# Two-layer decoder trunk with a routed expert mixer: order of x's reloads, of the scatters and of the gathers between the layers

## The reference, cut to what matters

```python
h = rms_norm(x, norm1_gain[l]);  z = h @ w_in[l]        # q, k, v, u: 512 columns each
att, pool = dilated_attention(q, k, v), pool_mixer(u, ...)
x = x + concat([att, pool]) @ w_out[l]
x = x + hier_moe(rms_norm(x, norm2_gain[l]), ...)        # each token goes to 2 of 16 experts
```

## Time and profile before

| | us |
|---|---|
| median of three runs | 1723.12 |
| the profiled execution | 1723.27 |
| its span, from the first instruction to the last | 1721.4 |
| PE busy | 1491.7 |
| DVE busy | 781.1 |
| ACT busy | 452.3 |
| POOL busy | 315.3 |

### The profile page before, as it was taken

The page is one execution under the profiler, slowest core; times in us unless marked ns, Lnnn a source line. Parts: engine busy times, 40 slices in busy tenths (PEclk is TensorE's granted clock), DMA queues, the critical chain, the costliest instruction groups (busy, mean ns, idle before and its releaser), DMA issues.

```text
span 1721.4 us, 22556 instructions
## 1 busy us (share of the span) xinstructions
PE 1491.7 (87%) x6963; PEld 1079.8 (63%) x6964; DVE 781.1 (45%) x1883; ACT 452.3 (26%) x886; POOL 315.3 (18%) x204
## 2 busy tenths in 40 slices
PE   5999978998992999999289998899999749999990
PEld 4878867886882444444178786788778624444440
DVE  5777656663336122212267866656533452212210
ACT  4231245662111011111222222567412101111110
POOL 1000068001000122222500001930200012222224
PEclk9999989999995999999599999899999869999995
DMA  8000020000168499973870002000002945999947
GB/s 314 19 1 0 0 98 1 2 1 1 73 222 291 156 283 298 341 223 89 226 222 0 1 0 98 1 1 2 1 25 90 330 154 160 270 301 280 311 91 162
DMA packets 116624, 221.09 MB, mean 128 GB/s; under 512 B 5976, under 2 KB 72736, under 8 KB 116544
## 3 DMA queue, kind: packets, MB, share of 16 engines
q1 hardware_dynamic: 91744, 131.82, 22.2%
q0 software_dynamic: 19136, 69.38, 16.4%
q10 hardware_dynamic: 5664, 18.88, 2.8%
HBM read 170.77 MB, written 49.28 MB: 128 GB/s over the span
## 4 chain that ended last, share of the span: by engine, by line
PE 77%; DVE 7%; issue 6%; DMA 3%; ACT 2%; POOL 1%; ACTq 1%; DVEq 0%; PEld 0%; PEldq 0%; POOLq 0%; SPq 0%
PE ps L1566 19%; PE ps L1360 17%; PE ps L1340 11%; PE ps L1493 9%; PE ps L1579 9%; PE ps L1446 7%; PE ps L1420 2%; DMA out_x<-x_res,arena 2%; PE ps L1507 2%; PE ps L1422 1%; POOL out_x L622 1%; DVE arena L1149 1%; PE ps L1480 1%; DVE w_in_lo L944 1%; DMA big<-in_w_in 1%
## 5 line engine op out<-in xcount | busy, mean ns | idle before, releaser
L1566 PE MATMUL ps<-big,arena 128*128 x720 | 325.8, 606 | 9.6 <-issue 8.3
L1340 PE MATMUL ps<-cst,arena 128*128 128x128 f32 x1242 | 186.4, 284 | 76.4 <-DVE arena L915 37.6
L905 DVE TENSOR_TENSOR arena<-ps,par 128x512 f32<-128x512 f32 x126 | 81.2, 686 | 355.8 <-PE ps L1340 355.8
L1566 PEld LDWEIGHTS ps<-big,arena 128*128 128x128 f32 x720 | 135.7, 194 | 170.4 <-issue 170.4
L1340 PEld LDWEIGHTS ps<-cst,arena 128*128 128x128 f32 x1242 | 152.6, 146 | 122.7 <-DVE arena L915 39.3
L1360 PE MATMUL ps<-w_in_hi,hT_hi 128*128 128x512 f32 x512 | 206.1, 402 | 12.7 <-DVE hT_lo L933 9.9
L1360 PE MATMUL ps<-w_in_hi,hT_lo 128*128 128x512 f32 x512 | 202.1, 395 | 0.0
L1360 PE MATMUL ps<-w_in_lo,hT_hi 128*128 128x512 f32 x512 | 201.9, 394 | 0.0
L614 POOL DMA_INDIRECT x_res<-token_rows,row_tok x62 | 61.0, 985 | 605.1 <-issue 309.2
L1579 PE MATMUL ps<-big,arena 128*128 x360 | 163.8, 598 | 5.4 <-issue 5.4
L1446 PE MATMUL ps<-big,arena 128*128 128x64 f32 x1152 | 149.7, 278 | 0.0
(11 more groups left out here) (169 smaller groups left out, 1770.1 us busy)
## 6 DMA issues: line engine op xcount, KB each, us to landing
big<-in_w_gate SPq DMA_DIRECT2D x32, 1024.0 KB, 10.6
big<-in_w_up SPq DMA_DIRECT2D x32, 1024.0 KB, 13.1
big<-in_w_down SPq DMA_DIRECT2D x32, 1024.0 KB, 15.3
big<-in_w_in SPq DMA_DIRECT2D x16, 1024.0 KB, 9.5
big<-in_w_out SPq DMA_DIRECT2D x4, 2048.0 KB, 10.3
token_rows<-arena ACTq DMA_DIRECT2D x16, 512.0 KB, 3.3
out_x<-x_res ACTq DMA_DIRECT2D x16, 512.0 KB, 4.1
x_res<-out_x SPq DMA_DIRECT2D x8, 512.0 KB, 5.8
```

What stands on the lines that cost most here:

```text
L905: ins = ve.tensor_tensor(out=dst[:, 4 * h:4 * h + 4, :], in0=ps[:, banks + h, :].rearrange("p (a c) -> p a c", c=P), in1=spread(gain[:, 4 ...
L1340: ins = te.transpose(ps[:, bank + i // 4, (i % 4) * P:(i % 4 + 1) * P], src, ident)
L1566: ins = te.matmul(ps[:, 2, :], xgT[:, k, :], big[:, ds(at + k * 2 * FE, 2 * FE)], start=k == 0, stop=k == K - 1)
```

## The change

SP's order between the layers is turned round: it now waits for the used blocks' scatters itself, loads x's tiles 0 and 1, steps the new semaphore `spare_may`, and only then loads the two parts of w_in. Tiles 2 to 4 wait for the gathers alone, tiles 5 to 7 for all scatters, and wpool comes last. ACT's Else branch waits for `spare_may` before it lets a spare scatter go. GpSimd waits itself, in every `add_rows` but block 0's, until all earlier scatters have landed, then steps `y_free` (which takes `y_whole`'s place for the evacuations of y) and waits for the two halves of y. The gathers get a bound on the row, and empty rows are given a row number above it, so that they are skipped. `y_whole` and `x_whole` are gone.

```diff
@@ -424,6 +424,7 @@
             sp.sem_inc(w_loaded, BIAS)
+            sp.sem_inc(spare_may, BIAS)
             sp.dma_start(xr[:, 0, :], x[0, 0:P, :]).then_inc(s_x[0], 16)
...
@@ -449,29 +450,34 @@
                     used = sp.value_load(start_i[0:1, NE:NE + 1], min_val=2 * SEQ // P, max_val=BLOCKS)
-                    sp.wait_ge(dn_done, upto(l, BLOCKS, used - BLOCKS))
-                    load_in(l, 1, 2)
-                sp.wait_ge(pm_done, upto(l, 2 * NG, 0))
-                sp.dma_start(wpool[:, :, :], w_pool[ds(l, 1), :, :, :].rearrange("a g c e -> c (a g) e"))\
-                    .then_inc(s_wpool, 16)
-                with sp.If(l > 0):
-                    sp.wait_ge(x_whole, upto(l, 1, 0))
+                    sp.wait_ge(s_add, upto_added(0, used))
                     sp.sem_inc(s_passed, 1)
                     for t in range(2):
                         sp.dma_start(xr[:, t, :], out[t * P:(t + 1) * P, :]).then_inc(s_again[t], 16)
+                    sp.sem_inc(spare_may, 1)
+                    sp.wait_ge(dn_done, upto(l, BLOCKS, used - BLOCKS))
+                    load_in(l, 1, 2)
                     for t in range(2):
                         sp.wait_ge(s_again[t], l * 16)
                         sp.sem_inc(x_ready, 1)
                     for i in range(RING):
                         sp.wait_ge(s_xg[i], l * (16 * USES[i]))
                         sp.sem_inc(s_passed, 1)
+                    for t in range(2, 2 + RING):
+                        sp.dma_start(xr[:, t, :], out[t * P:(t + 1) * P, :]).then_inc(s_again[t], 16)
+                    for t in range(2, 2 + RING):
+                        sp.wait_ge(s_again[t], l * 16)
+                        sp.sem_inc(x_ready, 1)
                     sp.wait_ge(s_add, upto_added(l, 0))
                     sp.sem_inc(s_passed, 1)
-                    for t in range(2, T):
+                    for t in range(2 + RING, T):
                         sp.dma_start(xr[:, t, :], out[t * P:(t + 1) * P, :]).then_inc(s_again[t], 16)
-                    for t in range(2, T):
+                    for t in range(2 + RING, T):
                         sp.wait_ge(s_again[t], l * 16)
                         sp.sem_inc(x_ready, 1)
+                sp.wait_ge(pm_done, upto(l, 2 * NG, 0))
+                sp.dma_start(wpool[:, :, :], w_pool[ds(l, 1), :, :, :].rearrange("a g c e -> c (a g) e"))\
+                    .then_inc(s_wpool, 16)
                 sp.wait_ge(rows_t, 1)
...
@@ -613,11 +620,17 @@
                         out=xg[slot], out_offset=None, in_=token_rows,
-                        in_offset=bass.IndirectOffsetOnAxis(ap=row_tok[:, j:j + 1], axis=0)).then_inc(s_xg[slot], 16)
+                        in_offset=bass.IndirectOffsetOnAxis(ap=row_tok[:, j:j + 1], axis=0),
+                        bounds_check=SEQ - 1, oob_is_err=False).then_inc(s_xg[slot], 16)
                 def add_rows(j):
-                    pool.wait_ge(y_whole, upto(l, BLOCKS, j + 1))
+                    if j:
+                        pool.wait_ge(s_add, upto_added(l, j))
+                    pool.sem_inc(y_free, 1)
+                    pool.wait_ge(y0_ready, upto(l, BLOCKS, j + 1))
+                    pool.sem_inc(s_passed, 1)
+                    pool.wait_ge(y1_ready, upto(l, BLOCKS, j + 1))
                     pool.sem_inc(s_passed, 1)
...
@@ -830,13 +843,8 @@
                     a_.wait_ge(dn_done, upto(l, BLOCKS, t + 1))
-                    a_.wait_ge(y_whole, upto(l, BLOCKS, t + 2 - RING))
+                    a_.wait_ge(y_free, upto(l, BLOCKS, t + 2 - RING))
                     sc.activation(y[slot][:, 512:1024], ps[:, 5, :], ACT.Copy).then_inc(y1_ready, 1)
-                    a_.wait_ge(y0_ready, upto(l, BLOCKS, t + 1))
-                    a_.wait_ge(y1_ready, upto(l, BLOCKS, t + 1))
-                    if not first(t):
-                        a_.wait_ge(s_add, upto_added(l, t))
-                    a_.sem_inc(y_whole, 1)
...
@@ -851,11 +859,11 @@
                         moe_down(t, slot, m)
-                        a_.wait_ge(s_add, upto_added(l, t + 1))
-                        a_.sem_inc(x_whole, 1)
+                        a_.wait_ge(y1_ready, upto(l, BLOCKS, t + 1))
+                        a_.sem_inc(s_passed, 1)
                     with a_.Else():
+                        a_.wait_ge(spare_may, upto(l, 1, 1))
                         a_.sem_inc(y1_ready, 1)
-                        a_.sem_inc(y_whole, 1)
...
@@ -1226,7 +1234,9 @@
                 dve.wait_ge(listed, upto(l, 1, 1))
-                ve.tensor_scalar(row_tok[:, :], ps[:, 2, 0:32], -1.0, 0.0, ALU.add, ALU.max).then_inc(rows_known, 1)
+                ch.link(ve.tensor_scalar(R("spare"), ps[:, 2, 0:32], 0.0, float(2 * SEQ), ALU.is_equal, ALU.mult))
+                ve.scalar_tensor_tensor(out=row_tok[:, :], in0=ps[:, 2, 0:32], scalar=-1.0, in1=R("spare"),
+                                        op0=ALU.add, op1=ALU.add).then_inc(rows_known, 1)
                 ch.link(ve.tensor_copy(start_i[:, 0:NE], R("start")))
...
@@ -1266,7 +1276,7 @@
                     dve.wait_ge(dn_done, upto(l, BLOCKS, t + 1))
-                    dve.wait_ge(y_whole, upto(l, BLOCKS, t + 2 - RING))
+                    dve.wait_ge(y_free, upto(l, BLOCKS, t + 2 - RING))
                     ve.tensor_copy(y[slot][:, 0:512], ps[:, 4, :]).then_inc(y0_ready, 1)
```

More of the change, by code:

```diff
@@ L298, in trunk @@
         gates_listed = sem("gates_listed")
-        y_whole = sem("y_whole")
-        x_whole = sem("x_whole")
+        y_free = sem("y_free")
+        spare_may = sem("spare_may")
         w_loaded = sem("w_loaded")
@@ L527, in _ @@
             pool.wait_ge(s_ms, 2)
-            for s in (x_ready, pooled, wo_split):
+            for s in (x_ready, pooled, wo_split, y_free):
                 pool.sem_inc(s, BIAS)
@@ L640, in _ @@
             for s in (params, q_high_in, k_high_in, win_top, gain_in, sd1, sqz_done, sdz, cat_top, v_copied, u_copied, t_evac, p_ready, pt0_ev, at_ev, sd2,
-                      ge_exp, dm_exp, silu_done, aT_ready, y1_ready, y_whole, x_whole):
+                      ge_exp, dm_exp, silu_done, aT_ready, y1_ready):
                 a_.sem_inc(s, BIAS)
```

## The result

The kernel after takes 1745.16 us (median of 7 runs, 1739.47 to 1751.66), the kernel before 1723.12 (7 runs, 1715.76 to 1735.55). The ratio is 1.0125, with a 95% interval from 1.0099 to 1.0151: slower, as forecast, by 22 us where 17 were forecast. The profiled execution of the kernel after took 1751.66 us, 6.5 above its median, so its stages are worth more here than its total.

What follows compares the result with a forecast made beforehand. PE carries 77% of the chain, so the change, touching no matmul, counts only where PE stands still. 1723.3 - 5.0 - 5.8 + 4.4 + 23.8 + 0.5 - 0.5 = 1740.7, forecast 1740 us, range 1729 to 1749.

Steps and rivals of the forecast that it cites:

- The end: After layer 1's last used scatter, eight spare scatters each wait for the one before: 23.8 us lost.
- A step: One spare scatter's landing (6.0 us) plus POOL's answer to the semaphore (0.87 us): 6.87 us, bounds 6.1 and 7.2.
- First gap: In front of layer 1: layer 0's last used scatter lands sooner without w_in beside it, table load at 840.5, 5.0 us gained.
- Second gap: PE's wait in front of x's tile 2 in layer 1 goes, with its clock loss: 5.8 us gained.
- the clock's 1.2: Time PE loses to its halved clock after waiting for tile 2, forecast to go: 1.2 us.
- Tile 5: Between the layers, PE waits 3.2 us for tile 5 behind the spare scatters, plus 1.2 for the clock: 4.4 us lost.
- Sum: Whole kernel: all gains and losses added to the profiled 1723.3 us give 1740.7 us, 1% slower.
- The rivals: Three other outcomes for the spare scatters' steps: slower still (1761 us, chance 0.07), about equal, or faster.
- the faster: Spare scatters with nothing queued behind land in 3.3 us, steps of 4.17 us, kernel 1712 us; chance 0.05.
- the equal one: Spare-scatter steps between 4.5 and 6 us, the end costing 2 to 16 us, kernel 1715 to 1729 us; chance 0.10.
- the break-even of 5.4 us: Spare-scatter step length below which the kernel gains, from eight steps and a landing against 48.0 us.

Runs made afterwards that it cites:

- before_waits: The kernel before, with only GpSimd's wait in every add_rows for all earlier scatters added: 1782.4 us, ratio 1.0329.
- after_spares_free: The kernel after, with GpSimd waiting for earlier scatters only in front of a used block's scatter: 1714.99 us, ratio 0.9956 to the kernel before.
- before_gathers_skip: The kernel before, with only the bounded gathers and their row numbers added: 1716.22 us, ratio 0.9961.
- before_x_first: The kernel before, with only SP's order changed (x's tiles 0 and 1 first, then w_in, wpool last): 1730.15 us, ratio 1.0050.
- after_scatters_skip: The kernel after, with a bound on the scatters so that empty rows are skipped, the wait kept: 1711.47 us, ratio 0.9951 to the kernel before.
- after_skip_edge: The kernel after with skipped scatter rows and DVE's loop jump moved from tile 2's normalisation to tile 1's gain: 1710.93 us, ratio 0.9929 to the kernel before.
- both_edge: The kernel after with skipped scatter rows, no wait for spare blocks and DVE's loop jump moved: 1695.22 us, ratio 0.9834 to the kernel before.
- before_scatters_skip: The kernel before, with only a bound on the scatters added so that empty rows are skipped: 1708.85 us, ratio 0.9919.

## Why the prediction was right

**The end.** Right, and it is the result. Forecast: a loss of 23.8 us; profiled: 26.1. A step is 7.0 us (seven landings of 5.9 to 6.1, as forecast at 6.0, and 1.04 from landing to next issue where 0.87 was forecast), and the last used scatter took 6.92 us, not 6.0. That before_waits, the wait and nothing else, costs 57 to 61 us, after_spares_free, its removal, gives back 30, and the bounded gathers by themselves gain 7 (before_gathers_skip), shows that it is the wait and not the bounds or the loads.

**First gap.** Right: the used scatter landed in 6.02 us, the table load came at 840.41 (forecast 840.5). That this second number fits to a tenth is luck: the scatter was issued 0.48 us earlier than the forecast had it, and from its landing to the table load were 7.6 us, not 7.2, since SP's two issues took 1.84 us in place of 0.85. That w_in could be moved at no cost was right in this kernel only. ACT waited 1.26 and 1.91 us for it, with DVE's part unharmed. What I did not see is that the added wait is what protects it: with the spare scatters dense, SP's order alone loses (before_x_first, 1.0050), and part of its gain is lost in after_spares_free.

**Second gap.** The step that failed. I took PE's 4.58 us in front of tile 2 to be all the late tile's, and forecast that they and the clock's 1.2 would go. Tile 2 was there in time (ACT squared it at 866.38, against 866.3 forecast), yet PE waited 3.69 us. DVE's jump back to its loop's start costs at least 3.35 us there; in the kernel before it lay hidden behind the late tile. The clock's part did go: the granted clock is 1.00 from 875 to 881 (0.50 from 882 to 884 in the kernel before), and from tile 2's transposition to tile 3's are 11.83 us in place of 13.46. So 2.6 us were gained (7.8 at tile 3 less 5.15) and not 5.8.

**Tile 5.** Right in kind, low in size: 6.7 us lost where 4.4 were forecast. The last spare scatter landed at 902.37 + 6.10 = 908.5, forecast 903.5. The two scatters beside loads account for 4.7 us: block 22 took 11.03 us next to w_in (forecast 9), block 25 9.63 next to tiles 2 to 4 (forecast 7). A start 0.4 us later, the longer answers and some landings above 6.0 add about 3. Against them stands a term that did not come: DVE's subtractions of w_in_lo, for which I had added 3.2 us, met hardly any scatter, since block 22 had held the queue back; POOL's instruction at 854.95 met only their last 0.3 us, and took 1.74. That block 24 landed at 861.18 (forecast 861.3), and so that tile 2 came in time, is thus two errors that cancel.

**Sum.** The terms forecast gave +17; the profile's own give -5.15 - 2.6 + 6.7 + 26.1 = +25.1, the two spans +28.3, the medians +22. The misses at tile 2 (3.2 us), tile 5 (2.3) and the end (2.3) all go the same way and don't cancel; the median stayed in the range because it was wide enough. **The rivals**: the faster and the equal one needed steps under 6 us, and none came under 6.6 with full rows. after_scatters_skip shows where they would have been right: with steps of 3.85 us the same program takes 1711 us, below the break-even of 5.4 us that the prediction gave. The Trainium skill's fit ("DMA: Bandwidth & Descriptors", "Anatomy of one DMA — SWDGE (gpsimd) path", 2.0 us plus the bytes over 436 GB/s) gives, by an estimate from it, 3.2 us for such a scatter. This case's trace disagrees: a lone scatter with add of 512 KB took 5.9 to 6.1 us in every spare step at the end. An empty one took 2.7; if that is taken for the fixed part, it is 0.7 us above the page's, and the part for the bytes is 3.3 us instead of 1.2.

## What to carry to other kernels

Where a semaphore wait stands between two DMAs, count the whole landing and the answer once a step: here 7.0 us in place of 1.9 to 3.2. Where the order isn't needed (here 17 scatters of which nobody reads a row), leave the wait out, or better the bytes. When the first of several causes of a stall is removed, count only up to the next one, and look for it where an idle time has no releaser: it may have been there all along. A transfer that is moved later can meet traffic that it used to be ahead of, so test an order alone, not only with the edits that came with it.

## What the runs showed of the hardware

The jump back to the start of DVE's long loop left DVE idle for 3.35 to 6.7 us with nothing to wait for; the idle time moved with the jump (after_skip_edge, both_edge). The two longest stood beside loads of 375 to 386 GB/s, but 3.35 us stood beside 3 and beside 201 GB/s, and 4.93 beside 4, so how traffic enters was not settled, nor what the engine does in that time. An accumulating scatter of 128 rows of 4 KB took 6.0 us alone, 9.6 to 11.0 beside 1.5 to 3 MB of loads, and 2.7 with all rows skipped. Beside nine full scatters, most of them two to three us apart, 1 MB of plain load took 23.8 us to land. DVE's subtraction holds up POOL's scatter instruction whether or not its rows move: 5.89 us in place of 1.58 in the kernel before, and 5.89 in before_scatters_skip, where the scatter was empty.
